# Bias rows spread over partitions, memory norm moved to packs 13 to 18, selection ended one pack earlier, in a two-block transformer kernel

## What is computed

```python
def hybrid_mixer(h, w_in, ..., w_out, rel_bias, layer_idx):
    proj = h @ w_in                       # 1024 -> 3656
    (aq, ak, av, bq, bk, bv, cq, ck, cv, iq, ik, iw) = jnp.split(proj, ...)
    o_a = diff_attention(aq, ak, av, lam, ..., rel_bias[:, :4])      # s + bias, causal, softmax
    o_b = dilated_attention(bq, bk, bv, rel_bias[:, 4:8])
    o_c = dsa_attention(cq, ck, cv, iq, ik, iw, rel_bias[:, 8:])     # top 128 keys by the indexer's score
    return jnp.concatenate([o_a, o_b, o_c], -1) @ w_out

def dsa_attention(...):
    logits = jnp.einsum('bqhd,bkd->bqhk', iqb, ik) * 64 ** -0.5      # the indexer
    score = jnp.einsum('bqhk,bqh->bqk', jax.nn.relu(logits), iwb)
    _, idx = lax.top_k(score, topk)
    ...
x = x + hybrid_mixer(rmsnorm(x, norm_mix), ...)
x = x + memory_attention(rmsnorm(x, norm_mem), rmsnorm(mem, norm_memkv), w_mq, w_mkv, w_mo)
```

## Time and profile before

| | us |
|---|---|
| runs, median (lowest to highest) | 2875.98 (2873.41 to 2878.74) |
| profiled execution | 2880.03 |
| its span, first to last instruction | 2877.9 |
| PE busy | 2761.0 (96% of the span) |
| DVE, ACT, POOL busy | 1174.5, 1033.3, 1122.4 |
| mean granted TensorE clock | 0.985 |
| DMA | 259.71 MB, mean 90 GB/s |

### The profile page before, as it was taken

The page is one execution under the profiler, slowest core; times in us unless marked ns, Lnnn a source line. Parts: engine busy times, 40 slices in busy tenths (PEclk is TensorE's granted clock), DMA queues, the critical chain, the costliest instruction groups (busy, mean ns, idle before and its releaser), DMA issues.

```text
span 2877.9 us, 35435 instructions
## 1 busy us (share of the span) xinstructions
PE 2761.0 (96%) x12322; PEld 2178.9 (76%) x12322; DVE 1174.5 (41%) x1916; ACT 1033.3 (36%) x1579; POOL 1122.4 (39%) x477
## 2 busy tenths in 40 slices
PE   7898999999999999989989999999999989999997
PEld 5666787888887888855868888888888754788886
DVE  3677533555535222237784222122221346422212
ACT  3355534444433232242313222232222457322222
POOL 2333442444454443521404444544445420444443
PEclk9999999999999999999999999999999999999998
DMA  4433331333232322331203333333333210233333
GB/s 122 106 101 99 105 98 47 92 95 102 88 117 87 103 91 91 118 94 49 87 8 103 101 95 98 106 96 101 95 97 107 87 52 1 74 101 95 95 103 102
DMA packets 77815, 259.71 MB, mean 90 GB/s; under 512 B 8919, under 2 KB 12503, under 8 KB 77608
## 3 DMA queue, kind: packets, MB, share of 16 engines
q1 hardware_dynamic: 68976, 242.77, 27.3%
q10 hardware_dynamic: 8760, 15.88, 2.4%
HBM read 252.59 MB, written 6.03 MB: 90 GB/s over the span
## 4 chain that ended last, share of the span: by engine, by line
PE 83%; DVE 5%; ACT 2%; issue 1%; ACTq 0%; DVEq 0%
PE ps L736 24%; PE ps L738 24%; PE ps L737 24%; PE ps L1268 1%; PE ps L1282 1%; PE ps L1296 1%; PE ps L1274 1%; PE ps L1083 1%; PE ps L1015 0%; PE ps L1025 0%; PE ps L948 0%; PE ps L949 0%; PE ps L950 0%; DVE products L2348 0%; PE ps L976 0%
## 5 line engine op out<-in xcount | busy, mean ns | idle before, releaser
L690 POOL TENSOR_TENSOR wlo<-raw,whi 128x1024 fp32r<-128x1024 f32 x453 | 1108.5, 2450 | 1716.5 <-ACT whi L1329 1715.9
L736 PE MATMUL ps<-lin_hi,whi 128*128 128x512 f32 x2208 | 869.3, 394 | 15.6 <-DVE waves_tmp L2289 6.6
L737 PE MATMUL ps<-lin_lo,whi 128*128 128x512 f32 x2208 | 862.2, 390 | 0.0
L738 PE MATMUL ps<-lin_hi,wlo 128*128 128x512 f32 x2208 | 861.9, 390 | 0.0
L1329 ACT ACTIVATE whi<-raw 128x1024 fp32r<-128x1024 f32 x455 | 476.5, 1053 | 552.1 <-PE ps L738 458.7
L736 PEld LDWEIGHTS ps<-lin_hi,whi 128*128 128x128 f32 x2208 | 416.5, 189 | 109.2 <-issue 15.7
L737 PEld LDWEIGHTS ps<-lin_lo,whi 128*128 128x128 f32 x2208 | 416.6, 189 | 88.1 <-issue 2.2
L738 PEld LDWEIGHTS ps<-lin_hi,wlo 128*128 128x128 f32 x2208 | 416.4, 189 | 87.3
L736 PE MATMUL ps<-act_hi,whi 128*128 128x512 f32 x880 | 342.6, 389 | 0.0
L738 PE MATMUL ps<-act_hi,wlo 128*128 128x512 f32 x880 | 342.4, 389 | 0.0
L737 PE MATMUL ps<-act_lo,whi 128*128 128x512 f32 x880 | 342.3, 389 | 0.0
(11 more groups left out here) (348 smaller groups left out, 2657.2 us busy)
## 6 DMA issues: line engine op xcount, KB each, us to landing
raw<-in_packs SPq DMA_DIRECT2D x459, 512.0 KB, 3.5
table<-bias_scratch ACTq DMA_DIRECT2D x12, 256.0 KB, 3.0
bias_scratch<-biasrow ACTq DMA_DIRECT2D x16, 160.0 KB
x<-in_x_t SPq DMA_DIRECT2D x4, 512.0 KB, 8.2
out_t<-x ACTq DMA_DIRECT2D x8, 256.0 KB, 2.2
bias_scratch<-biasrow ACTq DMA_DIRECT2D x4, 320.0 KB
mem<-in_mem_t ACTq DMA_DIRECT2D x4, 256.0 KB, 4.2
pool_count<-in_pool_count ACTq DMA_DIRECT2D x1, 1024.0 KB, 4.9
```

The costliest lines, as they stand in the source:

```text
L690: pool.tensor_tensor(wlo[:, n % 4, :], raw[:, n % 2, :], whi[:, n % 4, :].bitcast(F32), ALU.subtract).then_inc(low_split, 1)
L736: pe.matmul(target, wh, hi[:, k, :], start=(k == 0), stop=False)
L737: pe.matmul(target, wh, lo[:, k, :], start=False, stop=False)
L738: mm = pe.matmul(target, wl, hi[:, k, :], start=False, stop=(k == total - 1))
```

## The change

Five edits:

1. The 12 bias rows stand eight partitions apart, on 0, 8, ..., 88. `relb_apart` is a 32x96 matrix that is zero but for every eighth column, which DVE fills with 8 times `relb`. PE multiplies it as before (96 rows out). DVE adds a mask that is 96 rows high, cleared by a memset at the start; ACT waits for that memset before it loads the mask rows. The stores read every eighth partition. Their sizes, their number and their places are unchanged.
2. `mem` is loaded whole in one DMA behind pack 10, into other tiles. Its squares and high parts are made behind packs 13 to 16, its sums and low parts behind 14 to 17. DVE reads the sum behind pack 18, ACT takes the root behind pack 19.
3. The 48 rounds are spread over packs 8 to 28.
4. The tables of heads 0 and 1 are loaded at the end of ACT's piece behind pack 9.
5. `memory_root` is defined earlier, for edit 2.

```diff
 BIAS_A_AT, BIAS_B_AT = 2, 6
...
-MEM_LOAD_AT, MEM_AT, MEM_SUM_AT = A_FROM + 4, A_FROM + 6, A_FROM + 7
-TOP_FROM = 8
+MEM_AT = 13
+TOP_FROM, TOP_TO = 8, N_MIXER - 1
 
 
 def top_rounds(n):
 
-    slots = N_MIXER - TOP_FROM
-    return range(48 * (n - TOP_FROM) // slots, 48 * (n + 1 - TOP_FROM) // slots) if n >= TOP_FROM else range(0)
+    slots = TOP_TO - TOP_FROM
+    return range(48 * (n - TOP_FROM) // slots, 48 * (n + 1 - TOP_FROM) // slots) if TOP_FROM <= n < TOP_TO else range(0)
 
 
...
-    biasrow = put("biasrow", [12, WIDTH])
+    biasrow = put("biasrow", [12 * APART, WIDTH])
...
+    relb_apart = put("relb_apart", [32, 12 * APART])
+    maskrow = put("maskrow", [12 * APART, WIDTH])
     lamprod = put("lamprod", [P, 2, 64])
...
-    mem = nc.alloc_sbuf_tensor_at("mem", [P, DC, M], F32, offset=big_at + AK * T * 4)
+    mem = nc.alloc_sbuf_tensor_at("mem", [P, DC, M], F32, offset=big_at + BQ * T * 4)
...
-        pe.matmul(ps[0:12, 4, :], relb[:, :], onehot[:, 0:512], start=True, stop=True)
-        pe.matmul(ps[0:12, 5, 0:WIDTH - 512], relb[:, :], onehot[:, 512:WIDTH], start=True, stop=True).then_inc(bias_ready, 1)
+        pe.wait_ge(rel_apart, 1)
+        pe.matmul(ps[0:12 * APART, 4, :], relb_apart[:, :], onehot[:, 0:512], start=True, stop=True)
+        pe.matmul(ps[0:12 * APART, 5, 0:WIDTH - 512], relb_apart[:, :], onehot[:, 512:WIDTH], start=True, stop=True).then_inc(bias_ready, 1)
...
-            if fourth(n, MEM_SUM_AT) is not None:
-                mem_sum(fourth(n, MEM_SUM_AT))
+            if 0 <= n - MEM_AT - 1 < 4:
+                mem_sum(n - MEM_AT - 1)
...
+        act.wait_ge(mask_cleared, 1)
+        act.dma_start(maskrow[::APART, :], A["maskrow"]).then_inc(mixer_consts, 16)
...
-            rows = biasrow[heads.start:heads.stop, :].rearrange("h (o w) -> h o w", o=1)
+            rows = biasrow[APART * heads.start:APART * heads.stop:APART, :].rearrange("h (o w) -> h o w", o=1)
...
-        def load_memory(q):
-            act.wait_ge(mixer_maxed, 4 * q + 4)
-            act.dma_start(mem[:, 2 * q:2 * q + 2, :], A["mem_t"][:, 2 * q:2 * q + 2, :]).then_inc(mem_arrived, 16)
-
         def split_memory(q):
-            act.wait_ge(mem_arrived, 16 * (q + 1))
-            if q:
+            if q == 0:
+                act.wait_ge(mem_arrived, 16)
+                act.wait_ge(idx_added, 24)
+            else:
                 act.wait_ge(mem_sums, q)
...
-            if n == A_FROM - 1:
-                act.wait_ge(bias_a_stored, 16 * 4)
-                load_table(0)
-                load_table(1)
...
-            if fourth(n, MEM_LOAD_AT) is not None:
-                load_memory(fourth(n, MEM_LOAD_AT))
-            if fourth(n, MEM_AT) is not None:
-                split_memory(fourth(n, MEM_AT))
+            if n == MEM_AT - 3:
+                act.dma_start(mem[:, :, :], A["mem_t"]).then_inc(mem_arrived, 16)
+            if 0 <= n - MEM_AT < 4:
+                split_memory(n - MEM_AT)
+            if n == MEM_AT + 6:
+                memory_root()
...
+            if n == A_FROM - 1:
+                act.wait_ge(bias_a_stored, 16 * 4)
+                load_table(0)
+                load_table(1)
+
+        def memory_root():
+            act.wait_ge(mem_sums_read, 1)
+            order(act.activation(rstd_mem, rstd_mem, ACT.Ln))
+            act.activation(rstd_mem, rstd_mem, ACT.Exp, scale=-0.5).then_inc(mem_rooted, 1)
...
-            if s == 0:
-                memory_root()
...
+        dve.memset(maskrow[:, :], 0.0).then_inc(mask_cleared, 1)
...
+        order(dve.memset(relb_apart[:, :], 0.0))
+        dve.wait_ge(rel_arrived, 16 * 2)
+        dve.tensor_scalar(relb_apart[:, ::APART], relb[:, :], 8.0, None, ALU.mult).then_inc(rel_apart, 1)
...
-        order(dve.scalar_tensor_tensor(out=biasrow[:, 0:512], in0=ps[0:12, 4, :], scalar=8.0, in1=maskrow[:, 0:512],
-                                       op0=ALU.mult, op1=ALU.add))
-        dve.scalar_tensor_tensor(out=biasrow[:, 512:WIDTH], in0=ps[0:12, 5, 0:WIDTH - 512], scalar=8.0,
-                                 in1=maskrow[:, 512:WIDTH], op0=ALU.mult, op1=ALU.add).then_inc(biasrow_ready, 1)
+        order(dve.tensor_tensor(biasrow[:, 0:512], ps[0:12 * APART, 4, :], maskrow[:, 0:512], ALU.add))
+        dve.tensor_tensor(biasrow[:, 512:WIDTH], ps[0:12 * APART, 5, 0:WIDTH - 512], maskrow[:, 512:WIDTH], ALU.add).then_inc(biasrow_ready, 1)
...
-                memory_low(fourth(n, MEM_SUM_AT))
+            if 0 <= n - MEM_AT - 1 < 4:
+                memory_low(n - MEM_AT - 1)
+            if n == MEM_AT + 5:
+                dve.wait_ge(mem_sums, 4)
+                dve.tensor_scalar(rstd_mem, ps[:, STAT, 0:M], 1.0 / D, EPS, ALU.mult, ALU.add).then_inc(mem_sums_read, 1)
...
-            if s == 0:
-                dve.wait_ge(mem_sums, 4)
-                dve.tensor_scalar(rstd_mem, ps[:, STAT, 0:M], 1.0 / D, EPS, ALU.mult, ALU.add).then_inc(mem_sums_read, 1)
```

More of the change, by code:

```diff
@@ L111 @@
 KV_FROM = 2
+APART = 8
 BIAS_A_AT, BIAS_B_AT = 2, 6
@@ L266, in build_program @@
     relb = put("relb", [32, 12])
-    maskrow = put("maskrow", [12, WIDTH])
+    relb_apart = put("relb_apart", [32, 12 * APART])
+    maskrow = put("maskrow", [12 * APART, WIDTH])
     lamprod = put("lamprod", [P, 2, 64])
@@ L424, in build_program @@
     rel_arrived = sem("rel_arrived")
+    rel_apart = sem("rel_apart")
+    mask_cleared = sem("mask_cleared")
     gain_applied = sem("gain_applied")
@@ L1437, in _ @@
         act.dma_start(ident[:, :], A["ident"]).then_inc(ident_arrived, 16)
-        act.dma_start(maskrow[:, :], A["maskrow"]).then_inc(mixer_consts, 16)
+        act.wait_ge(mask_cleared, 1)
+        act.dma_start(maskrow[::APART, :], A["maskrow"]).then_inc(mixer_consts, 16)
         act.dma_start(diagmask[:, :], A["diagmask"]).then_inc(mixer_consts, 16)
@@ L1583, in pair_copy @@
                            ps[:, 4 + u % 2, 0:(qt + 1) * P].rearrange("p (b q) -> p b q", q=P), ACT.Copy).then_inc(mixer_copied, 1)
-        def memory_root():
-            act.wait_ge(mem_sums_read, 1)
-            order(act.activation(rstd_mem, rstd_mem, ACT.Ln))
-            act.activation(rstd_mem, rstd_mem, ACT.Exp, scale=-0.5).then_inc(mem_rooted, 1)
         for s in range(LAST_STEP):
```

## The result

The changed kernel took 2862.86 us (median of 5 runs, 2858.43 to 2863.8). The kernel before, run beside it, took 2878.74 (5 runs, 2873.41 to 2883.53). The ratio is 0.994, with a 95% interval of 0.9923 to 0.9957, so it is faster by 15.9 us. The profiled execution took 2862.86, of which 2860.8 is its span; the one of before took 2880.03 and 2877.94. So it is 17.2 us between the two profiles. Predicted were 2860.1 for the profiled execution and 2856 for the median.

What follows compares the result with a forecast made beforehand. PE's matmuls and PE's waits, mainly at pack 9 and the pair stage's start, bound the kernel. 13.6 - 1.0 - 0.3 + 8.8 - 1.2 = 19.9 us off 2880.03 gives 2860.1 profiled, median 2856; range 2850 to 2867.

Steps and rivals of the forecast that it cites:

- Pack 9: PE's stall there: stores from spread rows run faster, weight loads land sooner, relu waits go; 13.6 us gained, bounds 0 and 13.6.
- Rival 1: Bias stores before pack 9 run no faster, since the same DMA engines carry them; 13.6 us falls away, 2869.7; chance 8%.
- The edit's own costs: Spread rows at the kernel's start: extra DVE instructions and a new PE wait cost 0, or 0.3 us if cover fails.
- Edit 4: Tables loaded behind the indexer at pack 9, some 6 us later: worth 0, bounds -0.5 to 1.0 us.
- Memory's sums: Mid-mixer: three of PE's four sums merely trade steps; the fourth, formerly hidden in a wait, now costs 1.0 us.
- DVE's shortage: Packs 11 to 17: memory's parts and earlier selection rounds load DVE, costing 0.3 us, bounds 0 and -3.5.
- Rivals 2 and 3: Packs 11-17: DVE's shortage holds PE, 2863, 8%. Packs 13-16: PE, ACT and DVE take turns, 2879, 4%.
- Start of the pair stage: After the last tile: first pair's scores 5.4 us earlier, ACT's root 3.4 us off the chain; sum 8.8 us.
- What is given back: Pair stage: a drop of PE's clock may come again and reach beyond idle time; -1.2 us, bounds 0 and -5.0.

## Why the prediction was right, and where a term was off

**Pack 9 (predicted 13.6).** Measured 13.6 (13.96 - 0.33) in the profile, 12.0 and 13.1 us by the medians, with edits 2 to 4 absent and present. The reason holds: the bias rows' packets were slow because four neighbours share a path, the weight loads waited behind them, and ACT used up its lead. That they waited in the same DMA engines is inferred, since the trace doesn't name an engine: a quarter of the loads' packets waited until the store was over, and four packets of the store were under way at once, as on four engines of 16. The estimated pace, 16.5 to 19.6 GB/s an engine, was low (23.8). It was taken from other traffic; the prediction's other estimate, 12 and 3 us for a store, fits the packets, since 32 copies of a row take 12.0 us at 374 ns and 3.3 at 102. Landing times of 3.4 to 6.0 are shorter than the 7.2 to 10.6 I allowed; the kernel with rows two apart, at up to 8.9, shows that the step's time doesn't depend on this. Rival 1, that the same DMA engines limit the stores, has fallen. At every distance the trace holds 1580 packets of 2560 bytes, and in the stretch of the 320 KB stores mostly four of them are under way at once, as the engine count behind rival 1 has it; only their duration changed.

**The edit's own costs (predicted 0, or 0.3).** PE waits 0.8 us for `relb_apart` at 28 us, where it waited 1.4 for `sumsq` before:

```profile
PE ps L750 <- DVE sumsq L2012: 1.4, 1, 1.4
```

Nothing is lost. The memset is 0.14 us long on 96 columns.

**Edit 4 (0).** Right, by the kernel without it.

**Memory's sums and DVE's shortage (-1.0 and -0.3).** Up to tile 29 the profile has -2.6 + 0.25 + 0.85 = -1.5 for the two terms together, against -1.3. The near agreement hides a shift: the sum that no longer hides in a wait costs 0.9, against 1.0 predicted, but DVE's shortage costs nothing at packs 11 to 17, and the other 0.6 is DVE's delay with tile 22. DVE is short in the earlier steps, as the prediction had it (8.03 us step, 7.47 busy), and takes tile 15 3.6 us later behind tile 14 than before, but PE doesn't wait for it. Rivals 2 and 3 have fallen: PE's wait for DVE's maximum is 0.4 us as before (1.0 at most, in the kernel with edits 2 to 4 and the rows together), and it is PE's only wait between tiles 9 and 18, so ACT's split costs PE nothing.

**Start of the pair stage (8.8, and -1.2 for the clock).** Together 7.6 predicted, 8.56 measured. In the prediction's terms: the first pair's scores start 13.16 us sooner on DVE (264.67 against 251.51), of which 8.05 were there at tile 29, so 5.1 against 5.4. The remaining 3.4 is what the root was put at. Nothing was given back: the new kernel's fall of 3.4 us at 260.8 is matched by one of 3.4 us that the old one has at 292.1, and the lead stays 16.6 to 16.7 over both. On PE the same gain is 4.8 us less of waits (5.6 + 2.0 + 1.2 before, 1.0 + 0.4 + 2.6 now) and about 3.4 us of clock, which was at half for 10.2 us and is so for 3.4.

**The term that was mis-sized is the clock,** as the prediction put it: "What is given back", -1.2 at the pair stage, bounds 0 and -5.0. The loss came at packs 18 and 22 instead. The waits behind packs 18 and 22 were there before, in a profile in which the clock stayed full through both, and I never asked what else they could cost. At pack 18 it costs nothing or up to 3.4 us by the execution. Behind pack 22 edits 2 and 3 together make it dearer: one more round of selection and its threshold, stretched to 1.52 us, stand in DVE's step before a PE step that has lost memory's sum, tile 22 is taken 0.6 us late, and PE's wait grows from 2.5 to 3.1. With the longer falls of the clock that is an estimated 1.8 us that belong to the change. The prediction looked for DVE's shortage at packs 11 to 17 and not beyond.

The sum as measured is 0.3 + 13.6 - 1.5 - 2.8 - 1.6 + 8.6 + 0.5 = 17.1 us (start, pack 9, sums and DVE, clock at pack 18, clock at pack 22, pair stage, remainder to the end). Against the predicted 13.6 - 1.3 + 7.6 = 19.9 only the 4.4 us of clock are a large difference. More than half of that, pack 18's 2.8, is chance: in its second profile the changed kernel has no fall there and is 9.69 ahead at tile 23.

**From the profile to the median.** The predicted 2856 lay 4 below the predicted profile, because before's three runs shown had their median 4.05 below its profiled execution. Beside the changed kernel before had 2878.74, 2.8 higher. Of the miss of 6.9 us, 2.8 is this reference and about 4 the terms above: 19.9 predicted against 15.9 between the medians.

## What to carry to other kernels

A small store can hold up large loads: look at the time per packet of each queue, and if a source of a few long rows is slow, put the rows four partitions or more apart before anything else (a target of such rows was not tried). When a large wait goes, look at the small ones behind it, since one that costs 2.5 us of idle time may cost 3.4 more in clock, and a turn that writes into a bank which is still to be read can often stand a step later for nothing. To judge such a place, take more than one profile of the same kernel.

## What the runs showed of the hardware

- A DMA packet of 2560 bytes from one partition's row took 374 ns with four neighbouring rows in flight, 188 ns with two in a group of four partitions, and 102 ns with one. In every case a group of four partitions gave 25 to 27 GB/s. The 512 KB loads on another queue landed after 16, 6.0 and 3.5 us (medians) beside them; with the slowest store three quarters of a load's packets went on and one quarter began only when the store was over.
- A threshold instruction of VectorE on 128x384 took 0.36 us, but 0.75 and 1.52 us where it started while GpSimd's subtraction of 2.4 us was under way; both times it ended 0.2 us after that.
- After one and the same wait of TensorE of 2.5 us, behind pack 18, the granted clock stayed at 2.4 GHz in five of eleven profiles and fell to 1.2 GHz for 3.4 or 6.8 us in the others. With the wait of 3.1 us it fell in all six, and with waits of 5.8 us (pack 2) and 9.4 to 10.1 us (pack 9) in every profile that has them.
